# Fourier mixing and filter spectra from half tables, even tokens first

## The chip, the cores and the metric

The program runs on one core of one Trainium2 chip. The metric is the device time of one execution in microseconds, the median of several. Five engines work side by side and meet at semaphores: TensorE (PE) multiplies matrices into the eight banks of PSUM, ScalarE (ACT), VectorE (DVE) and GpSimd (POOL) work element by element, SyncE (SP) issues the DMAs.

## The reference, cut to what matters

Two networks of two layers follow one another on 512 tokens of width 1024, all in float32. The change lies in the first layer of the second network, in its mixer, which works on two sequences: x with L = 512 tokens and a context with L = 256.

```
def _fourier_hyena_mixer(h, ...):
    proj = h @ w_in                       # 512 Fourier columns and 3 x 512 others
    y_f = fft2(u_f, axes=(tokens, 128 channels of a group), norm='ortho').real
    x0, x1, v = split(dwconv3(...))
    spectrum = _hyena_filter_spectrum(L, ...)
    y_h = x0 * _long_conv(v * x1, spectrum, hy_bias)
    return concatenate([y_f, y_h]) @ w_out

_hyena_filter_spectrum: three layers h = sin(f * (h @ w + b)), then h @ w4, times a decay:
    h_fwd, h_bwd;  two_sided = [h_fwd, 0, reversed h_bwd[1:]] / sum(abs(two_sided));  rfft
_long_conv: irfft(rfft(u, n=2L) * spectrum, n=2L)[:L] + u * bias
```

## The kernel before, in words

Activations lie with features on the 128 partitions and tokens along the free axis: x in columns 0 to 511, the context in 512 to 767 (`groups`). Weights come from HBM in chunks of up to 2 MB through a ring of two slots; `PLAN` fixes their order, and one of its entries is the table `odd_dft_x`, in two chunks. Each `nc.Block()` is a stage: every engine has its own list of instructions in it, and the next stage begins when all have ended. Large products split float32 into a rounded part and a rest and make three fast matmuls; the matmuls of the two stages here are plain float32, which the profiler records as two matmul records each.

`fourier_hyena_layer` (L3833) runs in this order: the product with `fh_w_in`; `spectral_filters`; `spectral_products`; the product with `fh_w_out`.

`spectral_filters` (L3458), the filter stage, does three things at once on TensorE, in an order written out by hand at the end of its tensor part. (1) Fourier mixing: `first(u)`, 24 matmuls of 256 columns over the channels, and `second(m, half)`, eight mixings over the tokens (four groups of the context, then four of x), each as two halves, with tables `seq_dft` of all L token frequencies. (2) The filter network: `layer(l)` three times on TensorE, six chained VectorE instructions (L3666 to L3672), a sine on ScalarE (L3623). (3) Six token tiles (four of x, two of the context): `turn(i)` transposes a tile of v * x1, `side(i)` multiplies the last hidden layer with w4 into two banks, VectorE multiplies with the decay (L3679, L3680) and makes sum and difference (L3683, L3684), ScalarE takes absolute values (L3632), and `add_up(i)` on TensorE sums these over the partitions with one-column matmuls (L3564); VectorE waits for the sum before it overwrites the one buffer `sides`. At the end VectorE adds the sums and takes a reciprocal (L3689, L3690).

`spectral_products` (L3708) takes six steps of 128 frequencies (four of x, two of the context). In each TensorE makes four banks (L3750): the filter's real and imaginary part and those of the signal. ScalarE copies the filter's two banks (L3770, L3771), VectorE makes the complex product in six instructions, each waiting for the one before (L3792 to L3797). Two sets of four banks alternate. Then come the inverse transforms (L3760), four blocks of channels for each sequence; VectorE scales and adds the bias term (L3813), multiplies with x0 (L3815) and forms the rests (L3802) that the next product wants; ScalarE rounds (L3778, L3782). The next product begins with a rounding (L389) and a subtraction (L394) of its first weights.

## Time and profile before

| what | value |
|---|---|
| runs | 3637.9, 3639.84, 3633.84 us; median 3637.9 |
| the profiled execution's own time | 3633.4 us |
| its span | 3631.6 us |
| VectorE, ScalarE, GpSimd busy | 47%, 34%, 5% |
| HBM read | 303.6 MB, 84 GB/s over the span |
| mean granted TensorE clock | 0.986 |

The span is the time from the first to the last instruction in the profile. A granted clock of 1.0 is 2.4 GHz, 0.5 is 1.2 GHz. An engine's busy share over the whole span is a mean over many stages; here the two stages from about 2018 to 2222 us matter. A matmul's recorded duration includes its way through the array, so the pitch (the time from one to the next) is what it costs.

### The profile page before, as it was taken

The page shows a single profiled execution, that of the slowest core. Times are in us where ns is not written, and L with a number is a line of the kernel's source. Part 1 is how long each engine was busy: PE and PEld are TensorE (multiplying, and loading weights), DVE is VectorE, ACT ScalarE, POOL GpSimd, SP SyncE. Part 2 cuts the span into 40 slices and gives each one's busy share as a digit, 9 for nine tenths or more (in the row PEclk, how much of TensorE's full clock was granted, in tenths as well). Part 3 has the DMA queues.
Part 4 walks back from the last instruction along what each step waited for, and adds up shares of the span by engine and source line. Part 5 has one row for each costly group of instructions (what it writes and reads, how often), then busy time and mean ns, then how long its engine had stood idle before and what let it go on. Part 6 is the DMA issues. An engine that isn't in the chain of part 4 may idle for free. (4 is left out here: it accounts for less than half of the span.)

```text
span 3631.6 us, 45171 instructions
## 1 busy us (share of the span) xinstructions
PE 3491.4 (96%) x18104; PEld 2742.2 (76%) x18104; DVE 1717.8 (47%) x2996; ACT 1249.3 (34%) x2183; POOL 197.3 (5%) x258
## 2 busy tenths in 40 slices
PE   8999999999999999999999999999999988999999
PEld 6477887888766888788878546788888746777887
DVE  6544554333426854434366424544443536654543
ACT  3223433232336843323231212311122445642222
POOL 1041101000100011100000000000000111000000
PEclk9999999999999999999999999999999999999999
DMA  4276312222210031123221101111122310012222
GB/s 177 91 288 237 119 67 76 110 101 108 103 48 31 5 124 71 70 93 116 93 77 70 57 23 47 47 55 61 69 72 80 135 41 24 1 47 89 97 93 81
DMA packets 32174, 308.08 MB, mean 85 GB/s; under 512 B 4034, under 2 KB 7715, under 8 KB 11396
## 3 DMA queue, kind: packets, MB, share of 16 engines
q1 hardware_dynamic: 32004, 305.71, 23.3%
q8 instruction: 119, 1.95, 0.2%
q14 instruction: 51, 0.42, 0.0%
HBM read 303.60 MB, written 2.10 MB: 84 GB/s over the span
## 5 line engine op out<-in xcount | busy, mean ns | idle before, releaser
L717 PE MATMUL psum<-operand_rounded,weights_rest 128*128 128x512 f32 (+1 forms) x1328 | 501.0, 377 | 0.3
L718 PE MATMUL psum<-operand_rounded,weights_rounded 128*128 128x512 f32 (+1 forms) x1328 | 498.5, 375 | 0.0
L719 PE MATMUL psum<-operand_rest,weights_rounded 128*128 128x512 f32 (+1 forms) x1328 | 498.4, 375 | 0.0
L651 DVE TENSOR_TENSOR weights_rest<-ring,weights_rounded 128x1024 fp32r<-128x1024 f32 x160 | 199.7, 1248 | 399.4 <-ACT operand_rounded L612 399.4
L321 PE MATMUL psum<-operand_rounded,weights_rest 128*128 128x512 f32 (+1 forms) x1056 | 376.0, 356 | 6.3 <-DVE weights_rest L394 4.4
L322 PE MATMUL psum<-operand_rounded,weights_rounded 128*128 128x512 f32 (+1 forms) x1056 | 375.7, 356 | 0.0
L611 ACT ACTIVATE weights_rounded<-ring 128x1024 fp32r<-128x1024 f32 x160 | 169.2, 1058 | 434.0 <-PE psum L719 411.7
L717 PEld LDWEIGHTS psum<-operand_rounded,weights_rest 128*128 128x128 f32 x1328 | 250.5, 189 | 48.6 <-DVE weights_rest L642 3.1
L718 PEld LDWEIGHTS psum<-operand_rounded,weights_rounded 128*128 128x128 f32 x1328 | 250.5, 189 | 45.1 <-issue 0.5
L719 PEld LDWEIGHTS psum<-operand_rest,weights_rounded 128*128 128x128 f32 x1328 | 250.3, 188 | 45.3
L323 PE MATMUL psum<-h_rest,weights_rounded 128*128 128x512 f32 (+1 forms) x704 | 236.4, 336 | 0.0
L321 PEld LDWEIGHTS psum<-operand_rounded,weights_rest 128*128 128x128 f32 x1056 | 198.6, 188 | 39.0 <-DVE weights_rest L394 5.0
L322 PEld LDWEIGHTS psum<-operand_rounded,weights_rounded 128*128 128x128 f32 x1056 | 199.3, 189 | 28.9
L2783 PE MATMUL psum<-operand_rounded,weights_rest 128*128 128x512 f32 x512 | 200.8, 392 | 0.0
L2785 PE MATMUL psum<-operand_rest,weights_rounded 128*128 128x512 f32 x512 | 199.3, 389 | 0.0
L2784 PE MATMUL psum<-operand_rounded,weights_rounded 128*128 128x512 f32 x512 | 199.3, 389 | 0.0
L389 ACT ACTIVATE weights_rounded<-ring 128x1024 fp32r<-128x1024 f32 x88 | 92.4, 1052 | 248.7 <-PE psum L323 230.1
L323 PEld LDWEIGHTS psum<-h_rest,weights_rounded 128*128 128x128 f32 x704 | 132.3, 188 | 15.6
L323 PE MATMUL psum<-operand_rest,weights_rounded 128*128 128x512 f32 x352 | 137.6, 391 | 0.0
L321 PE MATMUL psum<-rounded,rounded 128*128 128x512 f32 (+1 forms) x384 | 129.9, 338 | 5.9 <-DVE rounded L394 4.6
L2835 DVE TENSOR_TENSOR weights_rest<-ring,weights_rounded 128x1024 fp32r<-128x1024 f32 x64 | 80.2, 1253 | 114.6 <-ACT weights_rounded L2804 114.6
L1160 PE MATMUL psum<-arena 128*128 128x256 f32 (+2 forms) x384 | 129.0, 460 | 5.2 <-ACT arena L1208 2.2
(504 smaller groups left out, 6452.6 us busy)
## 6 DMA issues: line engine op xcount, KB each, us to landing
ring<-in_ff_w SPq DMA_DIRECT2D x32, 2048.0 KB, 8.0
ring<-in_w_mod SPq DMA_DIRECT2D x24, 2048.0 KB, 8.2
ring<-in_ffn_up SPq DMA_DIRECT2D x22, 2048.0 KB, 8.0
ring<-in_ffn_down SPq DMA_DIRECT2D x33, 1024.0 KB, 4.9
ring<-in_xa_wk SPq DMA_DIRECT2D x4, 2048.0 KB, 8.0
ring<-in_xa_wv SPq DMA_DIRECT2D x4, 2048.0 KB, 8.4
ring<-in_xa_wq SPq DMA_DIRECT2D x4, 2048.0 KB, 8.0
ring<-in_xa_wo SPq DMA_DIRECT2D x4, 2048.0 KB, 7.9
```

Source lines behind the costliest of these rows:

```text
L321: nc.tensor.matmul(out, rest, top_in, start=(t == 0), stop=False)
L322: nc.tensor.matmul(out, top, top_in, start=False, stop=False)
L323: return nc.tensor.matmul(out, top, rest_in, start=False, stop=(t == kt - 1))
L611: act.activation(part("weights", "rounded", s, r, D), weight_rows(s, r), ACT.Copy).then_inc(rounded.sem, 1)
L651: dve.tensor_tensor(part("weights", "rest", s, r, D), weight_rows(s, r), part("weights", "rounded", s, r, D).bitcast(F32), ALU.subtract).t ...
L717: nc.tensor.matmul(out, rest, top_in, start=first and not behind, stop=False)
L718: nc.tensor.matmul(out, top, top_in, start=False, stop=False)
L719: mm = nc.tensor.matmul(out, top, rest_in, start=False, stop=last and (not behind or m % 2 == 1))
L1160: mm = nc.tensor.matmul(k.psum[:, base + cols.start:base + cols.stop], lhs, rhs, start=first, stop=last)
L2783: nc.tensor.matmul(k.bank(pos), rest[:, t, :], top_in, start=(t == 0), stop=False)
L2784: nc.tensor.matmul(k.bank(pos), top[:, t, :], top_in, start=False, stop=False)
L2785: mm = nc.tensor.matmul(k.bank(pos), top[:, t, :], rest_in, start=False, stop=(t == KT - 1))
```

## The change

Each table keeps half of its frequencies (or, for the way back, tokens), and the tokens are ordered even ones first, then odd ones. A transform is made as two: one over the even tokens and one over the odd; their sum gives one half of the outputs and their difference the other. In the mixing, `second` leaves both parts side by side in one bank, ScalarE copies them and GpSimd makes sum and difference. GpSimd also adds up the absolute values of the sides, over two buffers `sides`; eight one-column matmuls in the next stage sum the result over the partitions. The tokens of a tile are now every second one, so operands in SBUF are read with a step of two elements. The bias scaling on ScalarE comes first in `spectral_products`.

`spectral_products` has three steps instead of six. Each fills all eight banks (filter and signal, real and imaginary, even and odd tokens); ScalarE copies all eight and VectorE makes 24 instructions from the copies, with waits on its own earlier results. The inverse is made in three pieces: x from the first step's frequencies, the context, and x from the last step. `odd_dft_x` is one chunk of 2 MB instead of two, so the ring's slots swap for all later weights.

```diff
+    def tokens(gi, t):
+        half = nts[gi] // 2
+        lo = groups[gi][0] + 2 * P * (t % half) + t // half
+        return slice(lo, lo + 2 * P - 1, 2)
...
-                start = groups[gi][0]
-                nc.tensor.matmul(unit_bank(u), UF[:, g, start + t * P:start + (t + 1) * P], group_table, start=True,
+                nc.tensor.matmul(unit_bank(u), UF[:, g, tokens(gi, t)], group_table, start=True,
...
+                nt, n = nts[gi] // 2, groups[gi][1] // 2
+                table = seq_tables[gi][:, :, :].rearrange("p i (t n) -> p i t n", t=2 * nt)
...
-                for t in range(nt // 2 * half, nt // 2 * (half + 1)):
+                for j in range(nt):
+                    t = nt * half + j
                     for i in range(2):
-                        mm = nc.tensor.matmul(k.bank(6 + m % 2, n), waves(gi)[:, g, t, i * P:(i + 1) * P], rotated[:, i, t, :],
-                                              start=(t == 0 and i == 0), stop=(t == nt - 1 and i == 1))
+                        mm = nc.tensor.matmul(k.bank(6 + m % 2)[:, half * n:(half + 1) * n], waves(gi)[:, g, t, i * P:(i + 1) * P],
+                                              table[:, i, t, :], start=(j == 0 and i == 0), stop=(j == nt - 1 and i == 1))
...
+                if m >= 2:
+                    act.wait_ge(*halves_added.at(2 * (m - 1)))
+                nc.scalar.activation(halves[:, m % 2, 0:n], k.bank(6 + m % 2, n), ACT.Copy).then_inc(mixed_out.sem, 1)
...
+                fwd, bwd = sides[i % 2][:, 0, :], sides[i % 2][:, 1, :]
                 dve.wait_ge(*sided.at(i + 1))
-                if i:
-                    dve.wait_ge(*summed.at(i))
+                if i >= 2:
...
+        @block.gpsimd
+        def _(pool):
+            def add_halves(m):
+                gi, g = mixes[m]
+                start, n = groups[gi]
+                even, odd_half = halves[:, m % 2, 0:n // 2], halves[:, m % 2, n // 2:n]
+                pool.wait_ge(*mixed_out.at(m + 1))
+                pool.tensor_tensor(k.h[:, g, start:start + n // 2], even, odd_half, ALU.add).then_inc(halves_added.sem, 1)
+                pool.tensor_tensor(k.h[:, g, start + n // 2:start + n], even, odd_half, ALU.subtract).then_inc(halves_added.sem, 1)
+
+            def add_sides(i):
+                gi, t = tiles[i]
+                fwd, bwd, sums = sides[i % 2][:, 0, :], sides[i % 2][:, 1, :], added[:, gi, :]
+                pool.wait_ge(*absolute.at(i + 1))
+                if t == 0:
+                    pool.tensor_tensor(sums, fwd, bwd, ALU.add).then_inc(sides_added.sem, 2)
+                else:
+                    pool.wait_ge(*sides_added.at(2 * i))
+                    pool.tensor_tensor(sums, sums, fwd, ALU.add).then_inc(sides_added.sem, 1)
+                    pool.wait_ge(*sides_added.at(2 * i + 1))
+                    pool.tensor_tensor(sums, sums, bwd, ALU.add).then_inc(sides_added.sem, 1)
+
+            for m in range(4):
+                add_halves(m)
+            add_halves(4)
+            add_sides(0)
+            add_halves(5)
+            add_sides(1)
+            add_sides(2)
+            add_halves(6)
+            add_sides(3)
+            add_sides(4)
+            add_halves(7)
+            add_sides(5)
...
+    steps = [(1, 0), (0, 0), (0, 1)]
...
             for i, (gi, f) in enumerate(steps):
+                half = nts[gi] // 2
+                if i == 1:
+                    pe.wait_ge(*landed.at(16))
+                for b, (src, which, parity) in enumerate((src, which, parity) for sources in ((total, diff), (WT, WT))
+                                                         for which, src in enumerate(sources) for parity in range(2)):
+                    if i:
+                        pe.wait_ge(*copied.at(8 * (i - 1) + b + 1))
+                    for j in range(half):
+                        t = half * parity + j
+                        mm = nc.tensor.matmul(k.bank(b), there[gi][:, which, t, f * P:(f + 1) * P], src[gi][:, t, :],
+                                              start=(j == 0), stop=(j == half - 1))
+                    mm.then_inc(spectra.sem, 1)
+
+            def inverse(gi, f, c):
+                n = groups[gi][1] // 2
+                for r in range(2):
+                    for i in range(2):
+                        mm = nc.tensor.matmul(k.bank(4 * gi + c)[:, r * n:(r + 1) * n], spectrum[gi][f][r][i][:, c * P:(c + 1) * P],
+                                              back_again[gi][:, i, f, r * n:(r + 1) * n], start=(f == r == i == 0),
+                                              stop=(f == nts[gi] // 2 - 1 and r == i == 1))
+                return mm
+
+            pe.wait_ge(*copied.at(20))
+            pe.wait_ge(*multiplied.at(48))
+            for c in range(4):
+                inverse(0, 0, c)
+            pe.wait_ge(*copied.at(24))
+            for c in range(4):
+                inverse(1, 0, c).then_inc(back.sem, 1)
+            for gi in range(2):
                 for c in range(4):
+                    at = 384 + 4 * gi + c
+                    mm = nc.tensor.matmul(k.bank(7)[:, at:at + 1], added[:, gi, c * P:(c + 1) * P], k.c("ones", 0, 1), start=True, stop=True)
+            mm.then_inc(back.sem, 1)
+            pe.wait_ge(*multiplied.at(72))
+            for c in range(4):
+                inverse(0, 1, c).then_inc(back.sem, 1)
...
+            for i in range(3):
+                for b in range(8):
+                    act.wait_ge(*spectra.at(8 * i + b + 1))
+                    if i:
+                        act.wait_ge(*multiplied.at(24 * (i - 1) + 2 * (b // 2) + 2))
+                    nc.scalar.activation(copy[b], k.bank(b), ACT.Copy).then_inc(copied.sem, 1)
...
+            def step(out, a, b, op):
+                nc.vector.tensor_tensor(out, a, b, op).then_inc(multiplied.sem, 1)
+
+            dve.wait_ge(*biased.at(8))
             for i, (gi, f) in enumerate(steps):
+                def after(n):
+                    dve.wait_ge(*multiplied.at(24 * i + n))
+
+                (even_re, even_im), (odd_re, odd_im) = spectrum[gi][f]
+                if i:
+                    after(0)
+                for sums, differences, even in ((hp_re, hm_re, 0), (hp_im, hm_im, 2)):
+                    dve.wait_ge(*copied.at(8 * i + even + 2))
+                    step(sums, copy[even], copy[even + 1], ALU.add)
+                    step(differences, copy[even], copy[even + 1], ALU.subtract)
+                dve.wait_ge(*copied.at(8 * i + 6))
+                step(wp_re, copy[4], copy[5], ALU.add)
+                step(wm_re, copy[4], copy[5], ALU.subtract)
+                dve.wait_ge(*copied.at(8 * i + 8))
+                step(wp_im, copy[6], copy[7], ALU.add)
+                step(wm_im, copy[6], copy[7], ALU.subtract)
+                after(6)
+                step(yp, wp_re, hp_re, ALU.mult)
+                after(7)
+                step(tmp_p, wp_im, hp_im, ALU.mult)
+                step(ym, wm_re, hm_re, ALU.mult)
+                after(8)
+                step(tmp_m, wm_im, hm_im, ALU.mult)
+                after(10)
+                step(yp, yp, tmp_p, ALU.subtract)
+                after(12)
+                step(ym, ym, tmp_m, ALU.subtract)
+                step(wp_re, wp_re, hp_im, ALU.mult)
+                step(wp_im, wp_im, hp_re, ALU.mult)
+                step(wm_re, wm_re, hm_im, ALU.mult)
+                step(wm_im, wm_im, hm_re, ALU.mult)
+                after(16)
+                step(wp_re, wp_re, wp_im, ALU.add)
+                after(18)
+                step(wm_re, wm_re, wm_im, ALU.add)
+                step(even_re, yp, ym, ALU.add)
+                step(odd_re, yp, ym, ALU.subtract)
+                after(20)
+                step(even_im, wp_re, wm_re, ALU.add)
+                step(odd_im, wp_re, wm_re, ALU.subtract)
...
+            dve.wait_ge(*back.at(5))
+            last(nc.vector.reciprocal(flat(norm), k.bank(7)[:, 384:392]))
+            pieces = [(gi, c) for gi in (1, 0) for c in range(4)]
             for i, (gi, c) in enumerate(pieces):
                 s, n = groups[gi]
-                dve.wait_ge(*back.at(4 * gi + c + 1))
-                dve.wait_ge(*biased.at(4 * gi + c + 1))
+                dve.wait_ge(*back.at(i + 1 if gi else i + 2))
                 out = y[gi][:, c, :]
-                last(nc.vector.scalar_tensor_tensor(out=out, in0=k.bank(4 * gi + c, n), scalar=norm[:, gi, c:c + 1], in1=out,
+                last(nc.vector.scalar_tensor_tensor(out=out.rearrange("p (j r) -> p j r", r=2), in0=by_token(k.bank(4 * gi + c, n), n),
+                                                    scalar=norm[:, gi, c:c + 1], in1=out.rearrange("p (j r) -> p j r", r=2),
                                                     op0=ALU.mult, op1=ALU.add))
...
-PLAN += [("fh_w_in", KT, 512, 4), ("odd_dft_x", 4, 1024, 2), ("fh_w_out", KT, 512, 2)] + FFN(0)
+PLAN += [("fh_w_in", KT, 512, 4), ("odd_dft_x", 4, 1024, 1), ("fh_w_out", KT, 512, 2)] + FFN(0)
...
-        out["seq_dft_" + name] = np.stack([tiled(np.cos(ss) * norm), tiled(-np.sin(ss) * norm)])
-        th = np.pi * (np.outer(np.arange(n), 2 * np.arange(n) + 1) % (4 * n)) / (2 * n)
-        out["odd_dft_" + name] = np.stack([tiled(np.cos(th)), tiled(-np.sin(th)), tiled(np.cos(th).T / n), tiled(-np.sin(th).T / n)])
+        order = np.concatenate([np.arange(0, n, 2), np.arange(1, n, 2)])
+        out["seq_dft_" + name] = np.stack([tiled(np.cos(ss)[order, :n // 2] * norm), tiled(-np.sin(ss)[order, :n // 2] * norm)])
+        th = (np.pi * (np.outer(np.arange(n), 2 * np.arange(n) + 1) % (4 * n)) / (2 * n))[order, :n // 2]
+        out["odd_dft_" + name] = np.concatenate([tiled(np.cos(th)), tiled(-np.sin(th)), tiled(np.cos(th).T / n), tiled(-np.sin(th).T / n)], 1)
```

## Rows read from the trace of the kernel before

**Rows 1.** Engines' busy time, from the page: us (share of span) x instructions.

```profile
PE 3491.4 (96%) x18104; PEld 2742.2 (76%) x18104; DVE 1717.8 (47%) x2996; ACT 1249.3 (34%) x2183; POOL 197.3 (5%) x258
```

**Rows 2.** Busy time by stretch: the filter stage, the spectral products; then clock, DMA share, GB/s.

```profile
2017.64:2112.90 95.26, 85.91 (x301) 51.92 (x301) 32.46 (x45) 25.98 (x48) 0.00 (x0) 0.88 0.13 46
...
2112.90:2222.25 109.35, 104.76 (x256) 49.20 (x257) 42.78 (x66) 19.66 (x34) 0.00 (x0) 0.98 0.11 39
```

**Rows 3.** Timeline of TensorE, filter stage: start us, us, engine, line, operation [idle before].

```profile
2025.08 1.50 PE L3537 MATMUL psum<-h_all 33*64 33x512 f32 x4 [0.74 <-DMA h_all<-in_hy_w]
...
2033.52 5.38 PE L3522 MATMUL psum<-arena 128*128 128x256 f32 x16 [3.28 <-ACT h_all L3618]
...
2051.53 1.50 PE L3537 MATMUL psum<-h_all 64*64 64x512 f32 x4
...
2060.65 0.66 PE L3546 MATMUL psum<-const,arena 128*128 128x128 f32 x4
...
2061.23 1.98 PE L3557 MATMUL psum<-h_all 64*128 64x512 f32 x4
...
2102.59 1.98 PE L3557 MATMUL psum<-h_all 64*128 64x512 f32 x4
...
2108.37 3.57 PE L3564 MATMUL psum<-const,arena 128*128 128x1 f32 x16 [3.80 <-ACT arena L3632]
```

**Rows 4.** Timeline of TensorE, spectral products and the next product's first matmul.

```profile
2112.90 56.66 PE L3750 MATMUL psum<-arena,ring 128*128 128x512 f32 x128 [0.95 <-PEq L3487]
...
2183.13 27.63 PE L3760 MATMUL psum<-ring,arena 128*128 128x512 f32 x64
...
2210.59 7.07 PE L3760 MATMUL psum<-arena 128*128 128x256 f32 x32
...
2222.25 0.77 PE L321 MATMUL psum<-rounded,rounded 128*128 128x512 f32 x1 [4.59 <-DVE rounded L394]
```

**Rows 5.** GpSimd additions by line, whole span: duration min/median/max ns, first and last start.

```profile
L842 POOL TENSOR_TENSOR h_all<-h_all x42: 1278/1296/2369, 19.6 to 1516.1; 128x512 f32<-128x512 f32 x42
...
L2557 POOL TENSOR_TENSOR arena<-arena x14: 722/739/1534, 408.6 to 1330.7; 128x256 f32<-128x256 f32 x14
```

**Rows 6.** Timeline: a VectorE subtraction of 256 columns while GpSimd adds.

```profile
2811.05 1.52 DVE L653 TENSOR_TENSOR operand_rest<-arena,operand_rounded 128x256 fp32r<-128x256 f32 x1
```

**Rows 7.** Timeline of VectorE: two neighbours that don't wait for each other.

```profile
2064.73 0.69 DVE L3683 TENSOR_TENSOR arena<-arena 128x512 f32<-128x512 f32 x1
2065.34 0.68 DVE L3684 TENSOR_TENSOR arena<-arena 128x512 f32<-128x512 f32 x1
```

**Rows 8.** A VectorE group of chained products: busy us, mean ns, idle before us.

```profile
L3793 DVE TENSOR_TENSOR arena<-psum,arena 128x512 f32<-128x512 f32 x6 | 4.2, 692 | 0.2
```

**Rows 9.** Timeline of ScalarE: the eight bias scalings of the spectral products.

```profile
2180.86 4.14 ACT L3774 ACTIVATE arena<-arena,vec 128x512 f32<-128x512 f32 x8
```

**Rows 10.** Timeline of VectorE, end of the spectral products.

```profile
2187.78 3.56 DVE L3802 TENSOR_TENSOR h_rest<-h_all,rounded 128x768 fp32r<-128x768 f32 x4
...
2210.80 0.75 DVE L3813 SCALAR_TENSOR_TENSOR arena<-psum,arena 128x512 f32<-128x512 f32 x1 [4.79 <-PE psum L3760]
...
2212.79 0.48 DVE L3813 SCALAR_TENSOR_TENSOR arena<-psum,arena 128x256 f32<-128x256 f32 x1
...
2214.25 0.48 DVE L3813 SCALAR_TENSOR_TENSOR arena<-psum,arena 128x256 f32<-128x256 f32 x1
...
2218.56 0.99 DVE L3802 TENSOR_TENSOR h_rest<-h_all,rounded 128x256 fp32r<-128x256 f32 x2
```

**Rows 11.** A stretch after a stand of TensorE: busy times and granted clock.

```profile
2223.00:2225.00 2.00, 2.00 (x7) 1.52 (x6) 0.29 (x1) 0.00 (x0) 0.00 (x0) 0.50 0.03 8
```

**Rows 12.** VectorE groups that reduce out of PSUM with a stride.

```profile
L3689 DVE TENSOR_REDUCE arena<-psum 128x4 f32<-128x16 f32 x1 | 0.2, 175 | 4.8 <-PE psum L3564 4.8
L3689 DVE TENSOR_REDUCE arena<-psum 128x4 f32<-128x8 f32 x1 | 0.2, 167 | 0.0
```

**Rows 13.** Timeline: matmuls whose moving operand has a step of 64 bytes.

```profile
1039.86 1.01 PE L3081 MATMUL psum<-arena 128*128 128x124 f32 x4
```

More of the change, by code:

```diff
@@ L3631, in absolutes @@
                 act.wait_ge(*side_step.at(4 * i + 4))
-                nc.scalar.activation(flat(sides), flat(sides), ACT.Abs).then_inc(absolute.sem, 1)
+                both = flat(sides[i % 2])
+                nc.scalar.activation(both, both, ACT.Abs).then_inc(absolute.sem, 1)
             for u in range(8):
@@ L3684, in _ @@
[L3684 to L3690 removed]
+                nc.vector.tensor_tensor(total[gi][:, t, :], fwd, bwd, ALU.add).then_inc(side_step.sem, 1)
@@ L3754, in _ @@
-            pe.wait_ge(*landed[1].at(16))
-            for gi, (s, n) in enumerate(groups):
-                pe.wait_ge(*multiplied.at(30 + 6 * gi))
-                for c in range(4):
-                    for f in range(nts[gi]):
-                        for i, Y in enumerate((Yre, Yim)):
-                            mm = nc.tensor.matmul(k.bank(4 * gi + c, n), Y[gi][:, f, c * P:(c + 1) * P], table(gi, 2 + i)[:, f, :],
-                                                  start=(f == 0 and i == 0), stop=(f == nts[gi] - 1 and i == 1))
-                    mm.then_inc(back.sem, 1)
+                half = nts[gi] // 2
@@ L3818, in _ @@
                     rest_of(4 + tile, before[0], before[1], 4 + i)
-            rest_of(7, groups[1][0], groups[1][1], 12)
-    for s in range(2):
-        landed[s].base += 16
-    spectra.base += 12
-    copied.base += 6
-    multiplied.base += 36
-    back.base += 8
+            rest_of(7, groups[0][0], groups[0][1], 12)
+    landed.base += 16
+    spectra.base += 24
+    copied.base += 24
+    multiplied.base += 72
+    back.base += 9
     biased.base += 8
@@ L4524, in shape_constants @@
         decay = np.exp(-tt[:, None] * np.abs(deltas)[None, :])
[L4525 removed]
+        out["hy_decay_" + name] = tiled(decay[order])
     rows = np.repeat(np.arange(SEQ // GRID_W, dtype=f), GRID_W)
```

139 lines of the change are left out of this document (45 added, 94 removed).

## The prediction

> **What bounds the kernel now.** The page comes first: TensorE (PE) is busy 96% of the span [rows 1], so what a change is worth is mostly the TensorE time that it takes out, until another engine is late. The change touches two stages, so the view of stretches is next [rows 2]: the filter stage runs from 2017.64 to 2112.90 (95.3 us) and the spectral products from 2112.90 to 2222.25, where the next weight product begins (109.35 us). In the second, TensorE is busy 104.8 of 109.35 us and VectorE (DVE) 42.8: bound by TensorE. In the first TensorE is busy 85.9 of 95.3, at a granted clock of 0.88. The order of TensorE's work shows why [rows 3]: it waits for DMA and for the three layers of the filter network, and then makes six "side" tiles, from 2061.23 (first) to 2102.59 (sixth), one in 8.3 us, though a side is 1.9 us. In [rows 4] a matmul of 512 columns of plain float32 (two records each) costs 56.66/64 = 0.885 us with the slow beginning and 27.63/32 = 0.863 after it, one of 256 columns 7.07/16 = 0.442: the price follows the columns, so halving the columns or the tiles halves the time.
>
> **The change, part A: the filter stage.** TensorE loses the 48 sums of one column (six groups of 8 matmuls; the last is 3.57 us at the low clock, about 1.8 at the high one [rows 3]), their waits for the absolute values (3.8 us before the last), half the columns of the 48 mixing matmuls, and the low clock behind the sums. GpSimd (POOL) gets the sums of the sides (11 instructions of 512) and of the halves (8 of 128, 8 of 256).
> 1. Up to the third layer. The first layer waits for its DMA at 2025.08 and will again (a table load of 2 MB beside it is gone: at most 1 us earlier, kept for the range). The mixing of groups 2 and 3 of the short sequence waits until 2033.52 for ScalarE (ACT), which is busy with the first sine; it still will. These 8 matmuls took 5.38 us, mostly at the low clock; half as wide they take 8 x 0.22 x 2 = 3.5. So the second layer comes some 1.9 us earlier. Behind it the chain of VectorE and ScalarE is late, not TensorE: third layer about 2.8 us earlier, 2048.7 instead of 2051.53.
> 2. The first side is 9.7 us behind the third layer (2051.53 to 2061.23 [rows 3]), nearly all of it that same chain: 2058.4. TensorE has only 1.77 + 0.5 + 1.77 us of work meanwhile and stands some 3 us, so I charge a start at the low clock, +1.6: first side done 2061.8 (before: 2063.1).
> 3. Five tiles from there: half a mixing (4 matmuls of 256, 1.77), 4 transposes (0.5), a side (1.9) = 4.2 each, 0.5 less in the last: 20.5 us. Before 41.4 (2063.14 to 2104.5). Before, the transposes of the second tile began at 2060.65 and the side 0.58 behind them. VectorE needs 4 x 0.61 to 0.7 = 2.6 a tile and a side follows its second instruction, so it is not late. End of the sixth side: 2082.3, with about 0.7 for step 4: 2083.
> 4. GpSimd. A 512 add is 1.28 to 1.30 us, a 256 one 0.72 to 0.74 [rows 5]. From the end of a side to its finished absolute values is 3.8 us (2104.57 to 2108.37 [rows 3]). So from 2061.8 + 3.8 = 2065.6 it has 10 of 512 and 6 of 256: 10 x 1.33 + 6 x 0.75 = 17.8 us alone, inside the 21 of step 3 and ends at 2083.4. But VectorE and GpSimd delay one another: a VectorE subtraction of 256 columns of two SBUF operands, of which two take 0.99 us in [rows 10], took 1.52 beside a 512 add of GpSimd, and such adds reach 2.37 [rows 5, 6]. Of VectorE's four instructions a tile the last two are of this kind. If each of the 10 behind the first tile delays GpSimd by its 0.65, it has 24.3 us and ends at 2089.9. The other way: sixth side 2083, 3.8 to its absolute values, up to 1.3 for one add in VectorE's way, then two adds 2.7: 2090.8. I take 2091.6, as both meet, and 0.3 to the next stage: 2091.9. Gain 21 us of 95.3. Bounds: without any delay by one another 2087.5 (gain 25); with GpSimd at 1.7 and 1.0 in every add, between the ends of its rows, 16; at its dearest, 2.37 and 1.5, 9.
>
> The Trainium skill, "SBUF — State Buffer", section "Who interferes with whom", says that the pair of ports that VectorE and GpSimd share is an exclusive lock for the whole instruction, also against VectorE instructions with two SBUF inputs. The trace agrees in [rows 6] (1.52 is a wait for one add and then the work). By that rule step 4 is near its upper branch, not at 2087.5, which is where I have put it anyhow; it also says that VectorE's first two instructions of a tile, with one PSUM input, go free.
>
> **Part B: the spectral products**, time from the stage's start.
> 5. TensorE: forward 8 + 32 = 40 matmuls of 512 instead of 80: 34.4 us. Back: 32 of 256 (14.1) and 16 of 128 (halving again: 3.5), and 8 one-column sums (1.8). In all 54, before 105 (2112.90 to 2217.7). The start at the low clock stays (+1.6).
> 6. VectorE: 72 instructions of 512 instead of 36. Here they no longer wait for the one before but for one two places back, so I take the pitch of neighbours without a wait, 2064.73 to 2065.34 = 0.61 [rows 7]; each waiting for its predecessor costs 0.692 + 0.035 = 0.73 [rows 8]. It waits for 8 scalings on ScalarE first (4.14 us [rows 9]) and the first two copies: start 5.2. The first step is held back slightly by the copies behind TensorE (8 matmuls end at 8.5): done 20. Then 2 x 14.7: 34.9 and 49.6.
> 7. They mesh: TensorE's forward steps end at 8.5, 22.3 and 36.0; the inverse of the first half then needs VectorE's second step (34.9), so it starts at 36.0, then the short sequence and the sums: 48.6. VectorE's third step at 49.6 releases the last 7.07 us: TensorE done at 56.8. Nobody stands over 1 us.
> 8. VectorE's tail is now the path: 4 remainders of 768 (3.56), a reciprocal 0.25: 53.4; four pieces of the short sequence at 1.46 less the 0.26 by which a 256 remainder is shorter: 4.6; four of the long at 1.99: 8.0; the last remainder 0.4 to 0.7 [rows 10]: 66.4. TensorE's last result (56.8) is in time for them. Before, VectorE ended at 2219.55 (2218.56 + 0.99) and the next product began 2.7 us later [rows 4, 10]: so 69.1 us instead of 109.35, gain 40.2.
> 9. TensorE then has stood 12.3 us instead of 4.6. After 4.6 it ran at 0.50 (1.2 GHz) at 2223 to 2225 [rows 11]. How long it does after 12.3 no row shows; at worst as long again as after the stand before the filter stage. I take -1, bounds 0 and -2.5.
>
> Bounds of part B: every VectorE product at 0.73 instead of 0.61: +8.6, of which all is on the path. VectorE now reads the inverse result in PSUM with a stride in its last pieces. Nearest rows: a strided reduction out of PSUM of 16 elements takes 175 ns and one of 8 takes 167, 1 ns an element like a contiguous read [rows 12]; I take 0, upper end one more read time for each, 4 x 0.5 + 4 x 0.25 = +3. Below nothing: -1, if the copies are ready earlier. The nearest row to a matmul of 128 columns reads 124 at a step of 64 bytes: 2 are busy 1.01 us [rows 13], 0.5 each against my 0.22. For the 32 of them that is +9 at most; a gain beyond half the price of 256 columns is excluded by [rows 4]. The same row bounds the 60 operands in the filter stage that now take every second token (a step of 8 bytes: 24 first mixings, 24 transposes, 12 side matmuls): 60 x 0.28 = +17 at most, and no gain, since contiguous reads are no dearer in any row. I take 0 for both, the step being far from 64 bytes and the columns ruling in [rows 4].
> The Trainium skill, "Advanced Engine Details and Errata", section "Memory Cachelines", has lines of 16 bytes in SBUF and full speed from two hits in a line on; a step of 8 bytes has two, one of 64 has one. By that rule the 17 falls away and the sum stays; only the 64-byte row is shown by this trace.
>
> DMA: the seq table and the ring table halve and the second ring load goes; all landed in time before. The first chunk of the next weights is loaded at the start of the stage, the second at 56.8 and is wanted a full chunk later. Other stages only shift. Their ring slots swap, which is symmetric: 0.
>
> **Sum.** 21 + 40.2 - 1 = 60.2 us. The profiled execution took 3633.4 (span 3631.6), so 3573.2. The median of the three runs is 3637.9, 4.5 above it; on that scale 3577.7: I say 3578.
>
> **Rivals.**
> R1, GpSimd becomes the bound of the tiles: by its locked prices (the bounds in step 4) the filter stage gives 9 to 16 instead of 21: 3583 to 3590. For it: it has 18 to 24 us in a stretch of 21. Against: only two of VectorE's four instructions a tile meet it. Chance 0.13.
> R2, VectorE's products are dearer (0.73 and the strided reads): +8.6 + 3 = 3590. For it: with the tail VectorE is late everywhere from 49.6 on. Against: no wait for a neighbour. Chance 0.11.
> R3, better than forecast: no locks (25), the early DMA (1), no low clock at the first side (1.6): about 3571. Chance 0.12.
> R4, the other side: TensorE's low clock stays. Its granted clock fell to 0.5 after stands of 3 to 5 us, and the change makes more of them and less work between them. If both stages ran wholly at 1.2 GHz, TensorE's work, 54 us in products and some 47 in filters, would double, +101 less some 40 that hide in VectorE's time and in waits: 60 us, as much as is won; with stands on top, 3640 to 3655. It decides from about 60 us of extra work on the path. Against: in every row the clock is back within a few us of dense work, and the stages have dense work of 34 and 20 us. Chance 0.02.
> R5, the change does half of what it says (one stage's gain is lost to a wait that I have not seen, most likely the filter's 21): 3599. Chance 0.05.
> The forecast, 3578 with 3572 to 3584 of its own: 0.57.
>
> **How the numbers follow.** The range takes in R1 to R3 nearly whole: 3566 to 3596; beyond it lie R4, R5 and the worst of R2 with R1. About 0.2% (7 us) is what a measurement of this kernel can tell from no change. All cases but R4 is over 0.2% faster: faster 0.97, same 0.01, slower 0.02.
>
> **What would show it.** Right: no one-column sums in the filter stage; sides every 4.2 us; 16 + 11 adds on GpSimd, the stage 74 us long; in the products VectorE without a gap from 5 to 53 us, 0.61 apart; TensorE standing some 12 us before the next product; the stage 69 us. Wrong: sides over 5 us apart with VectorE waiting for GpSimd (step 4); pitch 0.7 in the products (step 6); matmuls of 128 columns at 0.4 (step 5); a granted clock of 0.5 beyond a few us (step 9).

## The result and the profile after

| | before | after |
|---|---|---|
| time, median of 4 (lowest to highest) | 3635.87 us (3633.62 to 3639.84) | 3577.11 us (3572.7 to 3582.72) |
| profiled execution: time, span | 3633.4, 3631.6 | 3572.7, 3570.9 |
| filter stage | 95.26 | 75.33 |
| spectral products | 109.35 | 69.34 |

The ratio is 0.984, 95% interval 0.982 to 0.986: faster by 58.8 us. 3578 was predicted. The span is shorter by 60.7 us; of this 19.9 is from the filter stage and 40.0 from the products. The rest is 1.2 us by which the filter stage began earlier (2016.47 instead of 2017.64), less some 0.4 lost behind the two stages, both in code that is the same in the two kernels.

The page of the changed kernel, engines' busy time, answers to [rows 1]. TensorE is busy as large a share as before, over a shorter span; GpSimd has 26 instructions and 23 us more:

```profile
PE 3415.7 (96%) x17944; PEld 2713.7 (76%) x17944; DVE 1740.9 (49%) x3030; ACT 1256.8 (35%) x2195; POOL 220.4 (6%) x284
```

Busy time by stretch, columns as in [rows 2]. The first two lines are the two stages; then the 9.3 us behind the stand ahead of the first side; then the first 6 us of the next weight product in three parts:

```profile
2016.47:2091.80 75.33, 57.56 (x204) 38.70 (x205) 36.02 (x42) 25.73 (x49) 23.70 (x26) 0.83 0.10 34
2091.80:2161.14 69.34, 56.07 (x192) 33.49 (x193) 61.43 (x103) 27.27 (x46) 0.00 (x0) 0.92 0.16 61
...
2055.22:2064.50 9.28, 9.28 (x20) 5.30 (x20) 2.64 (x4) 2.14 (x3) 1.34 (x3) 0.50 0.00 0
...
2161.14:2163.14 2.00, 2.00 (x5) 1.61 (x6) 1.04 (x1) 0.00 (x0) 0.00 (x0) 0.50 0.00 0
2163.14:2165.14 2.00, 2.00 (x8) 1.58 (x7) 0.00 (x0) 0.00 (x0) 0.00 (x0) 0.68 0.00 0
2165.14:2167.14 2.00, 2.00 (x11) 1.61 (x10) 0.00 (x0) 0.00 (x0) 0.00 (x0) 1.00 0.00 0
```

In the products TensorE is busy 56.1 of 69.3 us and VectorE 61.4: VectorE now bounds them. In the filter stage no engine is busy through: a chain across engines bounds it. TensorE's order of work in it (start, duration, engine, line, operation, idle before), against [rows 3]:

```profile
2046.11 1.50 PE L3543 MATMUL psum<-h_all 64*64 64x512 f32 x4 [0.53 <-ACT h_all L3614]
...
2055.22 1.13 PE L3551 MATMUL psum<-const,arena 128*128 128x128 f32 x4 [3.50 <-ACT arena L3619]
2056.28 3.78 PE L3561 MATMUL psum<-h_all 64*128 64x512 f32 x4
2059.99 3.78 PE L3528 MATMUL psum<-arena 128*128 128x256 f32 x8
2063.56 1.06 PE L3551 MATMUL psum<-const,arena 128*128 128x128 f32 x4
2064.55 2.41 PE L3561 MATMUL psum<-h_all 64*128 64x512 f32 x4
2066.89 1.99 PE L3528 MATMUL psum<-arena 128*128 128x256 f32 x8
...
2069.29 1.99 PE L3561 MATMUL psum<-h_all 64*128 64x512 f32 x4
...
2073.60 1.99 PE L3561 MATMUL psum<-h_all 64*128 64x512 f32 x4
...
2081.75 1.99 PE L3561 MATMUL psum<-h_all 64*128 64x512 f32 x4
```

The one-column sums (L3564 in [rows 3]) are gone. Sides follow one another 4.3 us apart at full clock (2069.29 to 2073.60). After a stand of 3.50 us everything costs double, until the second side is under way: sides of 3.78 instead of 1.99, a mixing of 3.78 instead of 1.99. The end of the stage is on VectorE and GpSimd; first VectorE, one instruction of the fifth side and the last two of the sixth, then GpSimd:

```profile
2080.54 0.74 DVE L3673 SCALAR_TENSOR_TENSOR arena<-psum,const,arena 128x512 f32<-128x512 f32 x1
...
2085.27 0.69 DVE L3676 TENSOR_TENSOR arena<-arena 128x512 f32<-128x512 f32 x1
2085.88 1.75 DVE L3677 TENSOR_TENSOR arena<-arena 128x512 f32<-128x512 f32 x1
```
```profile
2080.55 1.27 POOL L3697 TENSOR_TENSOR arena<-arena 128x512 f32<-128x512 f32 x1
...
2085.27 1.81 POOL L3694 TENSOR_TENSOR arena<-arena 128x512 f32<-128x512 f32 x1 [1.79 <-ACT arena L3624]
...
2088.18 0.72 POOL L3687 TENSOR_TENSOR h_all<-arena 128x256 f32<-128x256 f32 x1
2088.86 1.25 POOL L3697 TENSOR_TENSOR arena<-arena 128x512 f32<-128x512 f32 x1
2090.19 1.26 POOL L3699 TENSOR_TENSOR arena<-arena 128x512 f32<-128x512 f32 x1
```

VectorE's last subtraction takes 1.75 instead of the 0.68 that it took at 2062.19, before GpSimd's first add of a side, and GpSimd's add beside it 1.81 instead of 1.26. The instructions with one input in PSUM are not held up beside GpSimd: L3673 takes 0.74 at 2080.54, as at 2060.80 with GpSimd idle, and 0.68 at 2071.92, beside two GpSimd adds. The spectral products, first TensorE, against [rows 4], then VectorE, against [rows 7, 8, 10]:

```profile
2091.80 9.27 PE L3780 MATMUL psum<-arena 128*128 128x512 f32 x16 [8.06 <-PEq L3494]
2100.91 27.63 PE L3780 MATMUL psum<-arena,ring 128*128 128x512 f32 x64
2128.38 7.07 PE L3788 MATMUL psum<-ring,arena 128*128 128x256 f32 x32
2135.28 3.73 PE L3788 MATMUL psum<-arena 128*128 128x128 f32 x32
2138.85 1.84 PE L3803 MATMUL psum<-const,arena 128*128 128x1 f32 x16
2141.87 7.17 PE L3788 MATMUL psum<-ring,arena 128*128 128x256 f32 x32 [1.17 <-DVE arena L3831]
2161.14 0.77 PE L321 MATMUL psum<-rounded,rounded 128*128 128x512 f32 x1 [12.10 <-DVE rounded L394]
```
```profile
2096.99 2.61 DVE L3831 TENSOR_TENSOR arena<-arena 128x512 f32<-128x512 f32 x4 [9.36 <-ACT arena L3819]
...
2105.36 3.70 DVE L3831 TENSOR_TENSOR h_all<-h_all,arena 128x512 f32<-128x512 f32 x6
...
2139.32 2.50 DVE L3831 TENSOR_TENSOR arena<-h_all 128x512 f32<-128x512 f32 x4
...
2145.20 0.21 DVE L3885 RECIPROCAL arena<-psum 128x8 f32<-128x8 f32 x1
2145.45 0.48 DVE L3891 SCALAR_TENSOR_TENSOR arena<-psum,arena 128x256 f32<-128x256 f32 x1
...
2149.88 0.75 DVE L3891 SCALAR_TENSOR_TENSOR arena<-psum,arena 128x512 f32<-128x512 f32 x1
...
2156.97 1.47 DVE L3879 TENSOR_TENSOR h_rest<-h_all,rounded 128x512 fp32r<-128x512 f32 x2
```

From the stage's start at 2091.80, VectorE begins at 5.2, ends its 72 instructions at 50.0 and its tail at 66.6, with hardly a gap. TensorE's last result is there at 57.2 and it stands 12.1 us, at no cost to anybody.

### The profile page after: what moved, and what is told of

It is laid out like the page before. It is cut to its first block and busy times, and to the rows that moved or that the text cites. A ratio compares the mean times of both kernels' runs of the same rounds, so it can differ in the third digit from the quotient of the medians.

```text
span 3570.9 us, 44935 instructions
## 1 busy us (share of the span) xinstructions
PE 3415.7 (96%) x17944; PEld 2713.7 (76%) x17944; DVE 1740.9 (49%) x3030; ACT 1256.8 (35%) x2195; POOL 220.4 (6%) x284
## 5 line engine op out<-in xcount | busy, mean ns | idle before, releaser
L717 PEld LDWEIGHTS psum<-operand_rounded,weights_rest 128*128 128x128 f32 x1328 | 250.2, 188 | 48.9 <-DVE weights_rest L642 3.5
L321 PE MATMUL psum<-rounded,rounded 128*128 128x512 f32 (+1 forms) x384 | 129.6, 338 | 13.4 <-DVE rounded L394 12.1
```

Source lines behind the costliest of these rows:

```text
L321: nc.tensor.matmul(out, rest, top_in, start=(t == 0), stop=False)
L717: nc.tensor.matmul(out, rest, top_in, start=first and not behind, stop=False)
```

## The experiments

A kernel's median swings by several us from parts that no edit touches (last section), so the verdicts rest on the length of the two stages, from the stage's first matmul to the next stage's first matmul. Each is read from one profiled execution. Unchanged code gave 75.33 and 69.34, and in a second execution 74.93 and 70.19. The filter stage's beginning, up to the third layer, is no part of any edit but mixing_twice, and yet took 28.7 to 30.9 us in the twelve other profiled executions of the changed kernel and its variants. So the third column gives the filter stage from the third layer's first matmul on: 45.69 in the changed kernel, 61.37 in the one before. Medians of before were 3637.54, 3638.72 and 3637.67 in the three sets of runs, each on another chip.

| kernel | filter | from the third layer | products | median us | ratio, 95% |
|---|---|---|---|---|---|
| chained | 76.34 | 45.76 | 77.45 | 3587.36 | 0.986 (0.985 to 0.988) |
| forward_twice | 74.69 | 44.28 | 101.44 | 3609.74 | 0.993 (0.991 to 0.994) |
| mixing_twice | 81.29 | 48.27 | 68.66 | 3582.42 | 0.985 (0.984 to 0.987) |
| sums_on_tensor | 96.89 | 65.97 | 69.33 | 3600.43 | 0.990 (0.989 to 0.992) |
| differences_on_gpsimd | 75.03 | 44.17 | 75.29 | 3582.33 | 0.984 (0.983 to 0.986) |
| keep_clock | 70.16 | 41.31 | 69.12 | 3573.37 | 0.982 (0.981 to 0.984) |
| early_bias | 74.89 | 44.28 | 68.84 | 3575.48 | 0.983 (0.981 to 0.985) |
| early_bias_keep_clock | 70.06 | 41.32 | 68.09 | 3573.04 | 0.982 (0.981 to 0.984) |
| after_again | 74.93 | 44.18 | 70.19 | 3579.09 | 0.983 (0.981 to 0.984) |
| both_again | 72.04 | 41.32 | 69.37 | 3569.00 | 0.981 (0.980 to 0.983) |
| both_two_stands | 72.21 | 41.32 | 67.17 | 3569.23 | 0.981 (0.979 to 0.982) |
| halves_on_vector | 71.56 | 40.85 | 67.17 | 3573.71 | 0.982 (0.980 to 0.983) |

**What bounds the products.** Every VectorE product waits for the one before it:

```
 def step(out, a, b, op):
     nc.vector.tensor_tensor(out, a, b, op).then_inc(multiplied.sem, 1)
+    dve.wait_ge(*multiplied.at(next(each)))
```

> The changed kernel, but each of the 72 VectorE instructions of the spectral products waits for the one before it (as in the kernel before the change). Theory (VectorE sets the end of this stage): the pitch goes from 0.61 to 0.73 us, 72 x 0.12 = 8.6 less about 0.8 that the first step loses anyway to waits: the stage 69.3 + 8 = 77 us, the run some 3585. Rival (TensorE's halved work is still the bound and VectorE's is hidden): at most +1 us.

The stage took 77.45, 8.1 longer than in the changed kernel (7.3 longer than its second execution). The same six instructions as above took 4.32 us instead of 3.70, 0.725 apart instead of 0.605 (before's chained pitch was [rows 8]); each by itself still 0.69:

```profile
2114.07 4.32 DVE L3833 TENSOR_TENSOR h_all<-h_all,arena 128x512 f32<-128x512 f32 x6
```

So the 72 instructions are on the path, and the order of the change, in which each waits for one further back, is worth 7 to 8 of the 40 us. The other engine: the 40 forward matmuls made twice, so the spectra are made again for nothing.

```
-for j in range(half):
+for j in [*range(half)] * 2:
```

> The changed kernel, but every forward matmul of the spectral products is made twice (the second time over the first), so TensorE has the 80 of before again. Theory (TensorE was only just hidden behind VectorE, the halving is what made room): forward ends at about 70 instead of 36 us, VectorE's tail of the long sequence can't be covered any more, VectorE ends at about 98: the stage 100 us, +31, the run some 3608. Rival (VectorE alone sets the stage and TensorE has much room): +20 or less. Rival 2 (all 34.4 us of the added matmuls are on the path): +34.

101.44, 32.1 more for 34.4 us of added work: TensorE has little slack. The two engines mesh, as step 7 says; VectorE is just ahead.

**What the filter stage's gain is made of.** Two parts of the change there were undone one at a time: the mixing at its old price (its matmuls twice), and the sums of the sides back on TensorE (with the absolute values in two buffers as now).

```
-for j in range(nt):
+for j in [*range(nt)] * 2:
```

> The changed kernel, but every matmul of the Fourier mixing over the tokens is made twice, so that TensorE has the columns of before again. Theory (TensorE paces the six tiles): +8.9 us in the five tile periods (1.77 each), some 3 us before them, and some 4.5 less because TensorE no longer stands before the first side and so keeps its high clock there: the filter stage 75.3 + 7 = 82 us (+11 if the low clock stays). Rival (GpSimd paces the tiles): at most +4 in all.

```
+def add_up(i):
+    pe.wait_ge(*absolute.at(i + 1))
+    for c in range(4):
+        for b in range(2):
+            mm = nc.tensor.matmul(..., sides[i % 2][:, b, c * P:(c + 1) * P], k.c("ones", 0, 1), ...)
...
-            add_sides(i)   # GpSimd, all six
```

> The changed kernel, but the sums of the absolute values are made by TensorE again with six groups of 8 one-column matmuls in the places of before; the two buffers of sides stay, GpSimd keeps only the mixing's halves, the eight one-column matmuls of the next stage go. Theory: 5 x 1.84 us of matmuls on the path plus about 1.5 us of waiting for the absolute values in each tile (the halved mixing no longer covers it), a tail about 1 us shorter: the filter stage +15 to +20, 90 to 95 us. Rival (GpSimd's sums and their locks cost about what the one-column matmuls did): at most +5.

With before and after this makes a square (filter stage, us):

| | sums on TensorE | sums on GpSimd |
|---|---|---|
| mixing at full price | 95.3 (before) | 81.3 (mixing_twice) |
| mixing at half price | 96.9 (sums_on_tensor) | 75.3 (after) |

The 20 us are no sum of two gains. Halving the mixing while the sums stay brings nothing (-1.6): it saves 3.0 up to the third layer and costs 4.6 from there on (61.37 against 65.97). With the sums gone the halving brings 6. Moving the sums brings 14, and 21.6 with the half mixing. The lower left cell is not the old stage with half the mixing alone: the two buffers of sides and GpSimd's halves are in it too. sums_on_tensor missed its expectation (15 to 20). Where its 21.6 come from the groups of TensorE's instructions in the stage show (busy us, mean ns, idle before); first sums_on_tensor, then the changed kernel:

```profile
L3528 PE MATMUL psum<-arena 128*128 128x256 f32 (+1 forms) x96 | 29.3, 472 | 5.4 <-ACT arena L3623 5.0 <-ACT arena L3616 0.5
L3561 PE MATMUL psum<-h_all 64*128 64x512 f32 x24 | 18.4, 905 | 0.0
...
L3568 PE MATMUL psum<-const,arena 128*128 128x1 f32 x96 | 13.3, 269 | 4.3 <-ACT arena L3638 4.2
```
```profile
L3528 PE MATMUL psum<-arena 128*128 128x256 f32 (+1 forms) x96 | 23.4, 401 | 5.4 <-ACT arena L3609 5.0 <-ACT arena L3602 0.5
L3561 PE MATMUL psum<-h_all 64*128 64x512 f32 x24 | 14.1, 715 | 0.0
```

The sums themselves are 13.3 us. The same mixings and sides cost 5.9 and 4.3 more (29.3 against 23.4, 18.4 against 14.1): with the sums between them they run at the low clock for much of the time. From the first side to the end of the sixth the granted clock is 0.68, with TensorE busy 47.0 of 47.6 us; in the kernel before, with the same sums and the full mixing, it is 0.92. The clock's share was not in the expectation. Why small matmuls beside half the mixing keep the clock low, and beside the full mixing hardly, no run isolates.

mixing_twice shows the same from the other side. Its 4 added matmuls (8 records) keep TensorE at work where the changed kernel stands 3.50 us, and the first side takes 1.99 us, at full clock:

```profile
2059.53 3.62 PE L3528 MATMUL psum<-arena 128*128 128x256 f32 x16
...
2063.87 1.99 PE L3561 MATMUL psum<-h_all 64*128 64x512 f32 x4
```

**What locks would have cost in the products.** The 12 differences of copies go to GpSimd, beside VectorE's 60 others:

```
+for n, out in ((0, hm_re), (1, hm_im), (3, wm_im), (2, wm_re)):
+    pool.wait_ge(*copied.at(8 * i + 2 * n + 2))
+    pool.tensor_tensor(out, copy[2 * n], copy[2 * n + 1], ALU.subtract).then_inc(pooled.sem, 1)
```

> The changed kernel, but in the spectral products the 12 differences (four a step) are made by GpSimd beside VectorE, which keeps 60 of its 72 instructions. Theory (the two engines shut one another out when both read two SBUF operands): VectorE saves 12 x 0.61 = 7.3 us and is held up for up to 12 x 1.27 = 15 us: the stage 0 to 8 us longer, with single VectorE instructions of 1.2 to 1.9 us in the trace. Rival (they work side by side): VectorE's instructions all stay at 0.69, and the stage is some 2.5 us shorter, where TensorE's forward steps take over.

VectorE has 12 fewer instructions (7.3 us) and the stage is 6.0 us longer (5.1 against the second execution). VectorE's line first, then GpSimd's:

```profile
2107.21 1.76 DVE L3834 TENSOR_TENSOR h_all<-h_all,arena 128x512 f32<-128x512 f32 x1
2108.89 1.75 DVE L3834 TENSOR_TENSOR arena<-h_all,arena 128x512 f32<-128x512 f32 x1
...
2115.54 6.34 POOL L3903 TENSOR_TENSOR arena<-arena 128x512 f32<-128x512 f32 x2 [5.45 <-DVE h_all L3834]
```

Both lose: a VectorE instruction that meets a GpSimd one takes 1.75 instead of 0.68, and two GpSimd subtractions beside a busy VectorE take 6.34 instead of 2.5. Of these one took 4.67, the longest of its line, and the other 1.7, as most do. This is what the Trainium skill, "SBUF — State Buffer", section "Who interferes with whom", says (an exclusive lock for the length of an instruction), and the row gives it its price.

**The low clock.** TensorE makes matmuls whose result nobody reads, 8 in the stand ahead of the first side, 17 after the last side, 20 at the end of the products:

```
 second(5, 0)
+k.keep_running(pe, 2, 8)
 turn(1)
...
 side(5)
+k.keep_running(pe, 2, 17)
...
+pe.wait_ge(*last_step.at(2))
+k.keep_running(pe, 4, 20)
```

> The changed kernel with idle matmuls on constants into banks that nobody needs, in three stands of TensorE: 8 before the second transposes of the filter stage, 17 at its end, 20 at the end of the spectral products. Theory (the low clock after a stand lies on the path): -4.5 us at the first side and tile, -1 in the products, -1.5 in the next product: the run 7 us shorter, some 3570, the filter stage 71. Rival (the time lost at 1.2 GHz is hidden behind VectorE and GpSimd): the stages within 1 us of the changed kernel's.

The filter stage took 70.16, 5.2 less. Of this 0.8 lies ahead of the third layer, where the code is the same. From the third layer on, the stage takes 41.3 us in all four kernels with these idle matmuls and GpSimd's work as it was, and 44.2 to 45.8 in the six executions without them: they are worth 2.9 to 4.4 us. The first side is at full clock, 1.99 us instead of 3.78:

```profile
2052.41 3.62 PE L188 MATMUL psum<-const 128*128 128x256 f32 x16
...
2056.74 1.99 PE L3561 MATMUL psum<-h_all 64*128 64x512 f32 x4
```

The 17 make the first forward matmuls of the products faster (7.10 instead of 9.27 us). VectorE still starts at 5.2, held by ScalarE's bias scalings, but its first step now has no gaps and its 72 instructions end 48.9 us after the start instead of 50.0. The stage shows nothing of it (69.12), because the 20 idle matmuls at its end take it back: they end at 2154.69, VectorE at 2153.76. The bias scalings were moved into the filter stage, alone and with the idle matmuls:

```
 take_turned(5)
+bias_term(0)
 absolutes(4)
 take_mix(7)
 absolutes(5)
+bias_term(1)
```

> The changed kernel, but the eight bias scalings on ScalarE are made in the idle time of the filter stage's last tiles instead of at the start of the spectral products. Theory: VectorE starts at about 4 instead of 5.2 us, but the first step is then held by TensorE at its low clock, so the stage gains 0.5 us only. Rival (ScalarE's 4.1 us were on the path): -1.2 us or more.

> Both: early bias scalings and idle matmuls in the three stands. Theory: at the high clock the first spectral step comes as fast as VectorE takes it, which starts at about 2.4 us: the spectral products 2 to 2.5 us shorter than in the changed kernel, the run 8 to 9 us shorter, some 3568. Rival (VectorE's first step is bound by something else): as keep_clock.

Alone the move brings 0.5 in the products (68.84): now the copies behind the slow first matmuls are late. Together VectorE begins 2.7 us after the stage's start instead of 5.2. That the stage is not 2.5 shorter but 1.2 is, again, the 20 idle matmuls; the next part shows it.

**A version shorter in both stages, and what the last idle matmuls do.** The changed kernel again, this pair again, the pair without the 20 at the end, and the pair with the long mixing's halves on VectorE (GpSimd keeps the sums of the sides and the short sequence's halves).

> The changed kernel itself, on the chip of the next ones: 3577 within 3 us, the filter stage 75 and the spectral products 69 us.

> Early bias scalings and idle matmuls in three stands, unchanged from before. By the stage times seen (filter stage -5.3, products -1.3, next product no gain) it is 6.6 us faster than the changed kernel on the same chip, about 3570. Rival: the difference is lost in the variation of the stages outside, then within 2 us of it.

```
-pe.wait_ge(*last_step.at(2))
-k.keep_running(pe, 4, 20)
```

> As the one before, without the 20 idle matmuls at the end of the spectral products. Theory (they gave nothing, since TensorE still stands 2.7 us behind them and comes back at 1.2 GHz): stages and run the same as with them, within 1 us. Rival: they shorten the low clock of the next product, then 1 to 2 us slower there.

```
+if i in (0, 2, 3, 5):     # VectorE, after a side's own four
+    m = {0: 4, 2: 5, 3: 6, 5: 7}[i]
+    dve.tensor_tensor(k.h[:, g, start:start + n // 2], even, odd_half, ALU.add)...
+    dve.tensor_tensor(k.h[:, g, start + n // 2:start + n], even, odd_half, ALU.subtract)...
```

> As both_again, but sum and difference of the long sequence's four mixings (8 instructions of 256) are made by VectorE behind its tiles instead of GpSimd, which keeps the sums of the sides and the short sequence's halves. Theory (GpSimd is in time: the tail is the chain VectorE, absolute values, two adds): the filter stage within 1 us of both_again's 70. Rival (GpSimd's queue sets the end of the stage): 2.8 us or more shorter, the time of the four pairs.

The pair took 3569.0 us (3565.45 to 3574.29) and without the last 20 matmuls 3569.23 (3565.65 to 3573.66), the changed kernel 3579.09 (3569.19 to 3580.57) beside them. The medians are 10 us apart, but the runs overlap; the stages say 2.9 to 4.4 from the third layer on and, for both_two_stands against 69.34 and 70.19, 2.2 to 3.0 in the products. Its rows there:

```profile
2095.00 7.11 PE L3790 MATMUL psum<-arena 128*128 128x512 f32 x16 [0.92 <-PEq L3494]
...
2142.91 7.17 PE L3798 MATMUL psum<-ring,arena 128*128 128x256 f32 x32 [1.17 <-DVE arena L3838]
...
2162.17 0.76 PE L321 MATMUL psum<-rounded,rounded 128*128 128x512 f32 x1 [12.09 <-DVE rounded L394]
```

Why the 20 cost 2.2 us in both_again (69.37 against 67.17) its rows show. TensorE first, then ScalarE's start of the next stage; last, the same 20 in halves_on_vector, where they cost nothing (67.17):

```profile
2137.09 10.16 PE L3798 MATMUL psum<-ring,arena 128*128 128x256 f32 x32 [1.17 <-DVE arena L3840]
2147.09 8.80 PE L188 MATMUL psum<-const 128*128 128x256 f32 x40
2158.57 0.47 PE L321 MATMUL psum<-rounded,rounded 128*128 128x512 f32 x1 [2.69 <-DVE rounded L394]
```
```profile
2156.16 2.00 ACT L389 ACTIVATE rounded<-ring 128x1024 fp32r<-128x1024 f32 x2 [3.22 <-PEq L3769]
```
```profile
2148.86 8.80 PE L188 MATMUL psum<-const 128*128 128x256 f32 x40
```

VectorE had ended at 2153.66, but the stage ends only when TensorE's idle matmuls do, at 2155.89: 2.2 us later. In early_bias_keep_clock they end 0.9 us behind VectorE, and the stage is 0.9 longer than without them (68.09). In halves_on_vector they end at 2157.66, ahead of VectorE's 2158.40, and nothing is lost. The difference is the inverse before them, 10.16, 8.86 and 7.17 us at changing clock. What they buy is the clock: the next product's first matmul took 0.47 instead of 0.77, and its first output came 5.8 us after the start instead of 7.3. In three other profiled executions with these 20 the gain was nil. They are no bargain.

halves_on_vector was to bring the filter stage's end forward if GpSimd's queue set it. 71.56 against 72.04 and 72.21, from the third layer on 40.85 against 41.32: 0.5 us. Its median, 3573.71, is 4.7 above both_again's, with overlapping runs; in the profiled executions 5.2 us lie ahead of the filter stage (2022.38 against 2017.16).

## Why the prediction was right, point by point

The time came out 0.9 us from the forecast, inside every range, and both stages within 1.1 us of theirs. The mechanism held: the sums and half of the columns left TensorE, the end of the filter stage is VectorE's chain, and VectorE bounds the products. The closeness is in part luck. The runs of this kernel spread over 10 us, five later ones had a median of 3579.09, and inside the filter stage a miss of 2.5 us one way is in part taken back by misses of 1.5 and 0.8 the other. The steps:

- **Step 1** (third layer 2.8 us earlier): it came 29.6 us after the stage's start instead of 33.9, 4.3 earlier. Of the 1.5 beyond the forecast 1.3 are the stage's first 16 matmul records, the same as before, which took 5.39 us here and 6.70 before; in after_again they took 6.62, and the third layer came 3.1 earlier. So the step was right, and the 1.5 is this execution's.
- **Step 2** (first side at the low clock, +1.6; a gain of 1.3 to 1.4): the first side was done 43.6 us after the start instead of 45.6, a gain of 2.0. The stand was 3.50 us, as said. What failed is how long the low clock lasts: I had it for the first side alone, and it held for 9.3 us, over the next mixing and into the second side (for about 7 us in after_again, to the end of the mixing). The idle matmuls put its price at 2.9 to 4.4 us from the third layer on, against the 1.6 charged.
- **Step 3** (tiles of 4.2, the sixth side 20.5 + 0.7 behind the first): 4.3 at full clock, 23.7 in all. The 2.5 too many are that same low clock, the one term of the sum that was mis-sized. Step 1 gave part of it back: the sixth side ended 67.3 us after the start, against 65.4 forecast.
- **Step 4** (GpSimd and VectorE delay one another; the next stage 8.9 us after the sixth side): 8.1. Locked pairs are in the rows, 1.75 and 1.81. The branch in which VectorE's chain sets the end was the right one, though narrowly: the last absolute values ended at 2088.73 and GpSimd's queue was free at 2088.90. halves_on_vector takes the queue away and gains half a us. The bounds of this step don't follow from its terms. Without delay 2082.3 + 3.8 + 2.7 gives 2088.8 and not 2087.5. Ten adds at 1.7 and six at 1.0 from 2065.6 end at 2088.6, ahead of the other chain's end: nothing of the 21 is lost, where the step says that 16 are left. At 2.37 and 1.5 they end at 2098.3, a gain of 14 and not of 9. R1, priced from these bounds, was too dear. mixing_twice, in which the last adds meet no VectorE work (6.77 us of stand instead of 8.06), bounds what locks cost at the end at 1.3. The VectorE instructions with a PSUM input went free, at 0.68 to 0.74, as the lock rule named behind this step has it.
- **The operands of every second token** (0, up to +17): next to 0. Transposes take 0.63 for four against 0.60, sides 1.99 against 1.98, first mixings 3.73 for 16 records of 256 columns against 3.72. The rule of the Trainium skill, "Advanced Engine Details and Errata", section "Memory Cachelines", agrees with it.
- **Step 5**: forward 9.27 + 27.63, back 7.07 + 3.73 + 7.17, sums 1.84, in all 56.1 against 54; 128 columns are 3.73/16 = 0.23 a matmul, so the +9 bound was empty. The rest is the slow start, 9.3 for 8 matmuls.
- **Step 6** (start 5.2, pitch 0.61, done 20, 34.9, 49.6): start 5.2, pitch 0.605, third step done 50.0. chained shows that the pitch without a neighbour's wait was the choice that mattered, at 7.3 to 8.1 us (8.6 by the bound).
- **Step 7** (TensorE stands under 1 us): 1.17 us. forward_twice shows that it is right behind VectorE.
- **Step 8** (VectorE's tail to 66.4, next product at 69.1): 66.6 and 69.34. The strided reads of PSUM cost the same 0.48 and 0.75 as contiguous ones in [rows 10]: +0, and not the +3 of the bound.
- **Step 9** (-1 for the clock at the next product): after 12.1 us of standing it began at 0.50 and was back within 4 us, and its first output came 7.3 us after its start instead of 7.1: -0.2. The length of the stand did not matter.

R1 was ruled out by the rows of GpSimd (3 of its adds of sides over 1.3 us, none over 1.81; there are 10 of them, not the 11 that the last part counted) and by halves_on_vector. The dearer pitch of R2 is what chained built, and it was not there. Nor was R3: the locks and the low clock at the first side are both in the rows. But one of its terms was larger than it said, the low clock, at 3 to 4 us and not 1.6. R4 had its mechanism in the trace, 9.3 us at 0.50 in the filter stage, and sums_on_tensor shows a stage that runs much of its time that way; it stayed far from the 60 us at which it decides. R5: neither stage lost its gain.

## What to carry to other kernels

When TensorE's share falls in a stage, price the clock with the work: small matmuls that wait for another engine can cost nearly as much by what runs slowly between them as by themselves (10.2 us beside 13.3 in sums_on_tensor). A few idle matmuls inside a stand were worth 3 to 4 us here. At the end of a stage they must end before the engine that ends it: the last 20 did so in one profiled execution of four. Order a chain on VectorE so that each instruction waits for one two places back (0.605 us a piece here, and 0.725 with a wait for its neighbour). Split work between VectorE and GpSimd only where VectorE has pauses: beside a full VectorE both lose.

## What the runs showed of the hardware that was not expected

- The low clock does not last longer after a longer stand. After 3.50 us of standing TensorE, busy without a gap, was at 0.50 for 9.3 us in one execution and for about 7 in another of the same kernel; after the 12.1 us ahead of the weight product it was back in 4. The matmuls behind the two stands differ (plain float32 and rounded parts), and what decides it no run here isolates. Even the 1.17 us stand before the last inverse, after one-column sums, is followed by a slow piece in some executions: 10.16, 8.86 and 8.62 us instead of 7.17.
- A GpSimd instruction beside a full VectorE can wait for several of its instructions. In differences_on_gpsimd the longest took 4.67 us against 1.26 alone, while VectorE made six at its usual pitch. Most took 1.7.
- The runs of one kernel spread over 2.5 to 11.4 us, and between two profiled executions of the changed kernel, 6.8 us apart, 5.5 come from ahead of the two stages: the filter stage began at 2016.5 in one and at 2022.0 in the other. The offset grows step by step (2.5 us by 303 us, 4.1 by 901, 5.7 by 1329). What causes it stays open; no run was made for it.
